# Prompt's causal masks and forget sums entering the attention scores in single passes

## The reference, cut to what matters

```python
def fox_block(q, cq, qpos, k, v, ck_t, kpos):          # forgetting attention
    s = jnp.einsum('bqhd,bkhd->bhqk', q, k).astype(jnp.float32) * (HEAD_DIM ** -0.5)
    s = s + cq.astype(jnp.float32).transpose(0, 2, 1)[..., None] - ck_t[:, :, None, :]
    s = jnp.where((kpos[None, :] <= qpos[:, None])[None, None], s, -jnp.inf)
    p = jax.nn.softmax(s, axis=-1)
    return jnp.einsum('bhqk,bkhd->bqhd', p.astype(v.dtype), v)

def sb_block(q, qpos, k, v, kpos):                     # stick-breaking attention
    z = jnp.einsum('bqhd,bkhd->bhqk', q, k).astype(jnp.float32) * (HEAD_DIM ** -0.5)
    mask = (kpos[None, :] < qpos[:, None])[None, None]
    log_1m = jnp.where(mask, jax.nn.log_sigmoid(-z), 0.0)
    rest = lax.cumsum(log_1m, axis=3, reverse=True) - log_1m
    wgt = jnp.where(mask, jnp.exp(jax.nn.log_sigmoid(z) + rest), 0.0)
    return jnp.einsum('bhqk,bkhd->bqhd', wgt.astype(v.dtype), v)
```

## Time and profile before

| | |
|---|---|
| time of three runs | 2619.4, 2624.44 (median) and 2627.09 us |
| the profiled execution | 2623.07 us, of which 2621.4 us are the span from first to last instruction |
| TensorE busy in the span | 2534.5 us (97%), granted clock 0.989 of 2.4 GHz on the mean |
| DVE, ACT, POOL busy | 1325.9 us (51%), 914.9 us (35%), 204.2 us (8%) |
| stage 2 | about 494 to 926 us of the span |

### The profile page before, as it was taken

The page is one execution under the profiler, slowest core; times in us unless marked ns, Lnnn a source line. Parts: engine busy times, 40 slices in busy tenths (PEclk is TensorE's granted clock), DMA queues, the critical chain, the costliest instruction groups (busy, mean ns, idle before and its releaser), DMA issues.

```text
span 2621.4 us, 43516 instructions
## 1 busy us (share of the span) xinstructions
PE 2534.5 (97%) x16842; PEld 2331.3 (89%) x16842; DVE 1325.9 (51%) x1860; ACT 914.9 (35%) x1577; POOL 204.2 (8%) x320
## 2 busy tenths in 40 slices
PE   7999999999999979999999999999999999999998
PEld 7999998755565559999999999999999999999998
DVE  6345455334343456454554554554554554554555
ACT  5244455423232344332332332332332332332333
POOL 2060000133333300000000000000000000000000
PEclk9999999999999979999999999999999999999999
DMA  6293232699999932222222222222222222222222
GB/s 205 85 67 106 95 98 82 249 335 369 355 367 361 331 151 88 90 83 95 81 85 93 81 91 87 81 86 92 81 91 87 81 85 93 81 91 87 89 89 101
DMA packets 115362, 356.75 MB, mean 136 GB/s; under 512 B 30937, under 2 KB 39130, under 8 KB 90978
## 3 DMA queue, kind: packets, MB, share of 16 engines
q1 hardware_dynamic: 94402, 286.34, 33.1%
q0 software_dynamic: 20768, 67.65, 7.1%
HBM read 340.20 MB, written 13.74 MB: 135 GB/s over the span
## 4 chain that ended last, share of the span: by engine, by line
PE 85%; DVE 5%; issue 3%; ACT 3%; DMA 2%; SPq 2%; ACTq 0%; DVEq 0%
PE bank L419 48%; PE bank L424 24%; PE bank L1803 3%; PE bank L1745 2%; PE bank L1782 2%; DMA w_raw<-weights 1%; ACT w_hi L406 1%; DVE sum_tmp L488 1%; PE bank L1689 1%; PE bank L1684 1%; SPq L618 1%; SPq L622 1%; PE bank L1605 1%; ACT sum_tmp L482 1%; PE bank L1718 1%
## 5 line engine op out<-in xcount | busy, mean ns | idle before, releaser
L419 PE MATMUL bank<-x_act,w_hi 128*128 128x364 f32 (+1 forms) x4848 | 1061.9, 329 | 25.4 <-DVE x_act L500 13.1
L419 PEld LDWEIGHTS bank<-x_act,w_hi 128*128 128x128 f32 x4848 | 774.0, 189 | 28.0 <-issue 13.6
L419 PE MATMUL bank<-hid,w_hi 128*128 128x364 f32 (+1 forms) x3456 | 728.8, 329 | 18.6 <-DVE sum_tmp L488 17.6
L424 PE MATMUL bank<-x_act,w_lo 128*128 128x272 f32 x3232 | 650.5, 287 | 1.4 <-issue 1.4
L488 DVE TENSOR_TENSOR sum_tmp<-sum_tmp,bank 128x544 f32<-128x544 f32 x336 | 241.9, 720 | 723.2 <-ACT sum_tmp L482 723.2
L419 PEld LDWEIGHTS bank<-hid,w_hi 128*128 128x128 f32 x3456 | 555.0, 188 | 28.7 <-DVE sum_tmp L488 25.9
L424 PEld LDWEIGHTS bank<-x_act,w_lo 128*128 128x128 f32 x3232 | 563.1, 189 | 3.5 <-issue 2.2
L481 ACT ACTIVATE sum_tmp<-bank 128x184 f32<-128x184 f32 x336 | 108.7, 323 | 1021.9 <-PE bank L419 1021.8
L424 PE MATMUL bank<-hid,w_lo 128*128 128x272 f32 x2304 | 429.1, 287 | 0.0
L410 DVE TENSOR_TENSOR w_lo<-w_raw,w_hi 128x2048 fp32r<-128x2048 f32 x173 | 396.9, 2294 | 52.1 <-ACT w_hi L406 46.9
L424 PEld LDWEIGHTS bank<-hid,w_lo 128*128 128x128 f32 x2304 | 379.1, 188 | 0.0
(11 more groups left out here) (225 smaller groups left out, 1555.1 us busy)
## 6 DMA issues: line engine op xcount, KB each, us to landing
w_raw<-weights SPq DMA_DIRECT2D x173, 1024.0 KB, 4.8
k_ring<-fox_k SPq DMA_DIRECT2D x128, 256.0 KB, 5.1
v_ring<-fox_v POOLq DMA_DIRECT2D x128, 256.0 KB, 5.1
k_ring<-sb_k SPq DMA_DIRECT2D x128, 256.0 KB, 5.2
v_ring<-sb_v POOLq DMA_DIRECT2D x128, 256.0 KB, 5.4
wo<-w_early SPq DMA_DIRECT2D x16, 512.0 KB, 6.3
x_in<-xT SPq DMA_DIRECT2D x4, 1088.0 KB, 10.8
kv_out<-proj SPq DMA_DIRECT2D x4, 1088.0 KB, 9.8
```

Source lines behind the costliest of these rows:

```text
L419: ins = nc.tensor.matmul(bank[:, base + b, 0:n], hi, row[:, t:t + n], start=begin, stop=end)
L424: ins = nc.tensor.matmul(bank[:, base + b, 0:HALF], lo, row[:, t:t + HALF], start=False, stop=False)
```

## The change

The forget sums and the masks become operands of type `float32r`.

- The running sum goes to `pc[0:8]`. ACT copies it, rounded to `float32r`, to rows 0 to 7 of a new `c_prompt` of 72 rows, and DVE puts the difference between the sum and this high part into rows 64 to 71. POOL clears the 72 rows first. The weights are a new constant with a one in rows `h` and `64 + h`, so that one product adds both parts.
- The two masks become one constant of 129 columns, `diagonal`, read from column 0 for the forgetting attention and from column 1 for stick-breaking.
- ACT makes `float32r` copies of the identity, of `diagonal` and of `two_rows` in stage 1.

```diff
-_K = [("ident", P), ("ones", P), ("same_head", P), ("fox_mask", P), ("sb_mask", P),
-      ("pool_rec", GT * POOL_MAX), ("before", P), ("minus_one", 1)]
+_K = [("ident", P), ("ones", P), ("same_head", P), ("diagonal", P + 1),
+      ("two_rows", HEADS), ("pool_rec", GT * POOL_MAX), ("before", P), ("minus_one", 1)]
...
-    c_prompt = r.take("c_prompt", [HEADS, SEQ])
+    c_prompt = r.take("c_prompt", [HEAD_DIM + HEADS, SEQ], F32R)
...
# POOL, head of stage 2, before q_pad is cleared
+        nc.gpsimd.memset(c_prompt[:].bitcast(F32), 0.0).then_inc(c_cleared, 1)
...
# ACT, stage 1
+            if c == 4:
+                act.wait_ge(consts_in, 16)
+                f(ident_r[:], ident, ACT.Copy)
+                f(diagonal_r[:], cc("diagonal", 0, P + 1), ACT.Copy)
+                f(two_rows_r[:], cc("two_rows", 0, HEADS), ACT.Copy).then_inc(const_round, 1)
...
# ACT, head of stage 2
         for n in range(10):
             v_store(n)
+            if n == 4:
+                act.wait_ge(c_cleared, 1)
+                act.wait_ge(c_sum, 1)
+                f(c_prompt[0:HEADS], pc[0:HEADS], ACT.Copy).then_inc(c_high, 1)
...
# DVE, head of stage 2
-        v.tensor_tensor_scan(c_prompt[:], ones[0:HEADS, 0:1].to_broadcast([HEADS, SEQ]), logit[:, 0:SEQ], 0.0,
-                             ALU.mult, ALU.subtract).then_inc(c_ready, 1)
+        v.tensor_tensor_scan(pc[0:HEADS], ones[0:HEADS, 0:1].to_broadcast([HEADS, SEQ]), logit[:, 0:SEQ], 0.0,
+                             ALU.mult, ALU.subtract).then_inc(c_sum, 1)
...
# DVE, after the queries are padded
+        dve.wait_ge(c_sum, 1)
+        dve.wait_ge(c_high, 1)
+        v.tensor_tensor(c_prompt[HEAD_DIM:], pc[0:HEADS], c_prompt[0:HEADS].bitcast(F32), ALU.subtract).then_inc(c_ready, 1)
...
# TensorE, scores(i); const_round is waited for once before the loop
-            mm(s[0], ident[0:HEADS, h:h + 1].to_broadcast([HEADS, P]), c_prompt[:, 0:n], start=True, stop=False)
+            mm(s[0], two_rows_r[0:HEAD_DIM + HEADS, h:h + 1].to_broadcast([HEAD_DIM + HEADS, P]), c_prompt[:, 0:n],
+               start=True, stop=False)
...
-                mm(s[x][:, P * q:n], ident, cc(("fox_mask", "sb_mask")[x], 0, P), start=False, stop=True
+                mm(s[x][:, P * q:n], ident_r[:], diagonal_r[:, x:x + P], start=False, stop=True
                    ).then_inc((f_score, s_score)[x], 1)
...
-    put("fox_mask", np.where(j <= i, 0, MASKED).astype(np.float32))
-    put("sb_mask", np.where(j < i, 0, MASKED).astype(np.float32))
+    row, key = np.indices((P, P + 1))
+    put("diagonal", np.where(key <= row, 0, MASKED).astype(np.float32))
...
+    row, h = np.indices((P, HEADS))
+    put("two_rows", (row % HEAD_DIM == h).astype(np.float32))
```

More of the change, by code:

```diff
@@ L130, in build_step @@
     decay = r.take("decay", [P, 2, PAGE * 4 + NEW])
+    ident_r = r.take("ident_r", [P, P], F32R)
+    diagonal_r = r.take("diagonal_r", [P, P + 1], F32R)
+    two_rows_r = r.take("two_rows_r", [P, HEADS], F32R)
     r = Region(A_RAW, A_PROJ)
@@ L306, in build_step @@
     new_lf = sem("new_lf")
+    const_round = sem("const_round")
+    c_cleared = sem("c_cleared")
+    c_sum = sem("c_sum")
+    c_high = sem("c_high")
     c_ready = sem("c_ready")
@@ L1669, in _ @@
         pe.wait_ge(signs_in, 16)
+        pe.wait_ge(const_round, 1)
         pe.wait_ge(v_stored, 10)
```

## The result

The changed kernel takes 2641.4 us (median of 4 runs, 2639.9 to 2646.7), the kernel before beside it 2625.1 (4 runs): a ratio of 1.0079, 95% interval 1.0064 to 1.0094 (the two medians alone give 1.0062). It is 0.6 to 0.8% **slower**; 2615 had been forecast, with a range that ends at 2622. The profiled execution of the changed kernel is its longest, 2646.7.

The account below looks back on a forecast made before the run. TensorE, busy 97% of the span, was taken as the bound, with the key loads as the other clock; 7.5 + 2.0 - 0.3 = 9.2 us off the median 2624.44 gave 2615, range 2607 to 2622.

Parts of the forecast that it names:

- The prices: TensorE time saved in the attention stage: forget sums 0.25, 0.40, 0.57 and 0.72 us by key count, masks 0.21 us.
- The even stretches: Attention units i = 4n + 2 and 4n + 3: 0.94 us saved a period, 7.5 us in eight.
- the odd ones: Attention units i = 4n and 4n + 1: TensorE saves 1.07 us a period, of which only the keys' spare time is gained.
- the uncovered load: Weight load in each forget-sum product, 0.10 us a record: one record's share was kept; vanishing would save 0.10 more each.
- The rival that a narrow single-pass product isn't faster: Forget sums and masks: masks save nothing, the 128-key sum nearly nothing; 6.2 us gained, or 2618; chance 0.25.
- the sign of the penalty: Mask records in the profile after: a spacing of 0.2 us or more, not 0.11, would show narrow products slow.
- The work added at the head of stage 2: ACT's extra copy there pushes back the last value copies, 0.3 us lost; DVE's subtraction and POOL's clearing priced at nothing.
- i = 4n and 4n + 1: In these attention units key landings stay fixed, so 0.4 us is gained in five of eight periods, 2.0 us.
- a little: Deduction in units 4n and 4n + 1 for the next unit's values starting up to 1.07 us sooner and sharing the queue.
- Slower: Attention stage: earlier values push the last keys back; at a 6.5 us landing the kernel takes 2636; chance 0.05.
- The loads as a whole are the bound: Attention stage at DMA share 0.97: a shorter stage just has longer landings, gain 0 to 3 us, about 2623; chance 0.15.
- The keys keep up: Attention stage: keys land sooner as TensorE does, all 1.07 us gained in eight periods, 15.8 us, or 2608.6; chance 0.15.

Follow-up runs that it names:

- e7: The changed kernel plus 64 extra TensorE instructions before stage 3, half of the cached keys' loads left out; 2600.3 to 2614.6 us in five runs, stage 2 462.7 us.
- e1: The changed kernel with 64 more TensorE instructions (waits already met) at the head of stage 3; ratio 1.0027 to the kernel before.
- e14: The changed kernel with two idle products ahead of the forget sum of every unit 4n, before the release of the values; 2614.6 us.
- e13: The changed kernel with two idle products right ahead of the key products of every odd unit, after the release of the values; 2623.9 us.
- e15: e1 with POOL clearing an unused tile six times ahead of every odd unit's values, TensorE untouched; 2624.0 us, level with the kernel before.
- e6: The kernel before with half of the cached keys' loads left out, products still computed on old keys; stage 2 474.7 us.
- e11: e1 with the last page of values of each unit not loaded from the third unit on; ratio 1.0025.
- e10: The changed kernel with single-pass forget sums and masks for i = 4n + 2 and 4n + 3 only; 0.3% under the kernel before, stage 2 471.7 us.
- e2: The kernel before with 64 more TensorE instructions (waits already met) at the head of stage 3; 2643.0 us beside 2625.5.
- e8: The kernel before with the masks alone in single passes, forget sums unchanged; stage 2 482.7 us.

## Why the prediction was wrong

**The prices were right in kind, and what they save was put too low.** The even stretches gave 24.35 - 23.13 = 1.22 us a period where 0.94 was summed; the odd ones would give 21.68 - 20.30 = 1.38 (e7) where 1.07 was. The terms that were mis-sized are the records. In e7, where TensorE alone is the chain of the odd half too, the forget sums of 128, 256 and 384 keys take 0.06, 0.12 and 0.17 us, not 0.16, 0.22 and 0.27: the uncovered load vanished altogether, which the prediction had named as its cheaper case.

```profile
766.45 0.06 PE bank L1706
...
766.93 0.37 PE bank L1715 x2
773.35 0.12 PE bank L1706
```

The rival that a narrow single-pass product isn't faster is refuted: the two masks take 0.36 or 0.37 us where their four records took 0.64. But they don't come at 0.11 us as the transposes do. All 32 pairs start 0.16 us apart, between the 0.11 that was forecast and the 0.2 that was to be the sign of the penalty. The work added at the head of stage 2 cost what was allowed for it: from POOL's first clearing to TensorE's first sequence product it was 0.2 us more.

**The step that failed is that of i = 4n and 4n + 1.** The sum took the landing of the keys as fixed and let 0.4 us through in five periods, +2.0. It named the way in which this fails, the values that start up to 1.07 us sooner, and wrote it off as "a little", with 0.05 for the rival in which it decides. The values did start 1.4 us sooner (V 18.0, then 16.6), and the last keys landed 1.3 us later on average in the changed kernel (21.8, then 23.0), 0.6 in e1. e14 against e13 shows that this start, not TensorE's time, moves them, and e15, where only the start was moved, shows it again. The argument against that rival, a window at 413 GB/s, says that the engines can move more than the mean; it doesn't say whose packets wait. The odd stretches so became 8.9 us longer in the changed kernel (3.4 in e1), where 2.0 was to be saved. That alone would only have eaten the 8.5 us that the even stretches gained.

**What no term held: the clock behind a wait.** The sum priced a wait at its length, and so did the rival "Slower": by its own rule a landing 5.3 us behind the issue, the mean of the changed kernel, costs 8 x 0.3 us on balance. In the changed kernel six of the eight sets of key products behind a wait took 4.4 to 4.7 us in place of 3.1 (by the table's measure); over all sets it is 59.1 - 51.4 = 7.7 us, nearly all of the 8.1 by which the total grew. That the waits are the cause is what e6 (no waits on keys: 50.1 us) and e13 (an idle product in the gap: 52.1) show.

**What was nowhere in the prediction: stage 3.** Its 14.2 us are the larger part of the loss, and they come from 192 instructions fewer ahead of a loop. By the ratios the shift is worth 1.0079 - 1.0027 = 0.5%, or 14 us, in the changed kernel (9 by the medians, 11.5 by stage 3 of the two traces), and 0.6% in the one before (16.4 us by stage 3). No row of before shows it, since before had no such stop.

**The rivals.** "The loads as a whole are the bound" gave the right size of the gain for stage 2 before the clock, about nothing, for a wrong reason: e11 moves fewer bytes for no gain, and e10 moves all of them 7 us faster than before and 9 faster than e1. The means over the periods (first key products to eight microseconds before the last; before, changed, e10) show the room:

```profile
503.00:893.00 390.00, 383.54 (x2619) 217.66 (x2620) 160.60 (x426) 122.17 (x350) 126.98 (x236) 1.00 0.98 358
```

```profile
505.30:903.00 397.70, 370.67 (x2551) 208.76 (x2549) 160.47 (x426) 122.17 (x350) 128.30 (x239) 0.98 0.98 354
```

```profile
499.60:882.00 382.40, 368.74 (x2573) 213.66 (x2574) 160.54 (x426) 122.24 (x350) 127.10 (x236) 1.00 1.00 365
```

e10 moves 365 GB/s at a DMA share of 1.00, so there were 2% in hand; that more is left no run shows. The rule of the Trainium skill that stood beside that rival ("DMA: Bandwidth & Descriptors", the section on where 436 GB/s comes from) holds the loads of one core at about 358 GB/s, which it gets as half of what a memory stack gives two cores. The trace of before agrees to the figure, with its 358. e10's 365 over 382 us does not, in a kernel that runs on one core alone.

"The keys keep up" is refuted: where TensorE needs less time, the last keys land later (21.8, then 23.0), not sooner.

Open is why the order matters as much as it does: 1.1 us of earlier values made the keys 1.3 us later in e13 against e14, and 1.4 us made them 0.6 later in e1 and 1.3 in the changed kernel. That two queues share the 16 engines in the last stretch is shown; in what order their packets are served was not measured. Landings for the same start also differ between executions (22.3 to 23.0 us at V = 16.6), and that is unexplained.

## What to carry to other kernels

Where two queues load for one engine, that engine's own progress releases the transfers: before work is taken off it, ask which transfer starts sooner and what lands beside it. Here the half of the period in which nothing was late took the cheaper products for 0.3%, and the whole of it gave the gain back. After any edit that changes how many instructions an engine runs ahead of a loop, compare the loop's passes in both traces before explaining the total by the edit; padding the stream by some instructions, in both kernels, tells the two apart.

## What the runs showed of the hardware

A loop can lose 0.5 to 1.6 us behind each jump back by its place in the instruction stream alone: 2625.5 became 2643.0 us in the kernel before with 64 instructions that do nothing. The six stops are 7.5 us in the changed kernel and 6.8 in e2, and stage 3 is 14.2 and 16.4 us longer; the rest, 1.1 to 1.6 us a stop, fits the lower clock that was seen behind one of them (0.52), but was not added up.

In the changed kernel the key products behind an odd stretch of 22.5 us or more took 4.4 to 4.7 us, those behind the two of 22.0 and 22.3 us 3.0; TensorE's own work in it is 20.3 (17.9 in the first period). With an idle product in the gap stretches of up to 23.8 us were followed by 3.0, and the one of 24.6 by 5.7. The length alone doesn't decide: in e8 22.85 us was followed by 4.7 and 22.90 by 3.0.

Single-pass products of 128 columns are cheaper than two-record ones of the same width, 0.36 us a pair where it was 0.64, but their starts are 0.16 us apart, more than the 0.11 of the transposes. The forget sum of 384 keys took 0.17 us in the chain, and that of 128 keys 0.06.
